# Attention in a diffusion backbone layer: the joint item of the four context heads moves from the middle of its group to the end of it

## The chip, the cores and the metric

The kernel runs on one core of a Trainium2 chip. Five engines of that core matter here: TensorE (PE, with PEld for its weight loads), VectorE (DVE), ScalarE (ACT), GpSimd (POOL) and SyncE (SP, which issues most DMAs). Each runs its own instruction stream and waits on semaphores that the others raise. The metric is the device time of one execution in microseconds. Before the change the median of 3 runs is 1314.7 us (1314.26 to 1314.91).

## The reference

One layer of a hybrid backbone for 512 latent tokens and 128 context tokens, D = 1024, 8 heads. After modulation and norm, one input projection feeds a gated convolution and a differential attention; both are merged, and a two-level routed mixture of experts follows. The part around the change is the attention: two softmaxes per head over the same keys, of which the second is subtracted with a factor.

```
def diff_attention(q, k, v, lam):          # q, k: (tokens, 8 heads, 2, 64)
    s = einsum('bqhcd,bkhcd->bchqk', q, k) / sqrt(64)
    p = softmax(s, axis=-1)
    a = p[:, 0] - lam * p[:, 1]
    return einsum('bhqk,bkhv->bqhv', a, v)  # v: (tokens, 8 heads, 128)
```

Latent queries (4 tiles of 128) attend to 640 keys: the 512 latent ones and 128 cached context ones. The 128 context queries attend only to their own 128 keys.

## The kernel before, in words

The kernel is written engine by engine, with semaphores by hand; no scheduler reorders anything. The heads are handled in two groups of four. A group first makes its queries and keys (line 1481, with the transposes at 1488), then runs attention, and then the next group begins. After group 1 the feature products (line 1595) follow; then the output projection, the router and 16 experts.

The attention of a group is a pipeline over 17 items. Sixteen are long items: one head times one tile of 128 latent queries, against 640 keys, with both softmaxes. One is the context item: all four heads of the 128 context queries together, against 128 keys. The place of the context item in the group is the constant `CTX_AT` (line 95), which `item(n)` (line 99) and `long_items(n)` (line 105) read; every engine's loop asks `item(n)` which kind item n is. Items are numbered 0 to 16 within a group here.

What one item costs each engine, with the lines:

- PE: scores into one half of a two-part PSUM area (L1532, four matmuls for a long item; L1523, eight small ones for the context item), transposes of the mixed probabilities (L1559, four; a long item has a fifth, L1565), and the product with the values (L1577, five matmuls of a long item; L1570, four of the context item).
- DVE: the maxima (L1051 long, L1047 context), the mix of the two softmaxes (L1032, L1033, L1036 long; L1022, L1023, L1027, L1029 context, which form one chain in which each waits for the one before), and the copy of the result out of PSUM with the scaling (L1016 long, L1013 context).
- ACT: the exponentials with their row sums (L767, two of 640 columns for a long item; L760, eight of 128 columns for the context item), and the copies of the transposed probabilities to SBUF (L743 for the first four, L747 for the fifth).

The order of the work is set by three loops. At its turn m, PE does:

```
transposes of item m (waits for its mix)
if m + 3 < ITEMS: scores(m + 3)        # waits for the exponentials of m + 1
fifth transpose of m, if long          # waits for the first copy of m
values product of m                    # waits for the result copy of m - 1
```

DVE goes round with the result copy of m - 3, the maxima of m, and the mix of m - 1. ACT does the first copy of m - 2, then the exponentials of m with the fifth copy of m - 2 inside them: after the first of two in a long item, after the second of eight in the context item (L756, L765). All three queues run in order.

After item 16 of group 0, PE waits until the last result is copied (line 1581) and then starts the queries of group 1. After item 16 of group 1 it does not wait for that: the next instruction is a transpose of a packed table (L1584), which waits only for something done long before, and then the feature products (L1595) begin.

Of the kernel before, what the change touches and what calls it, by code (L numbers as in the profile page):

```python
# [91 lines left out]
    return j if 0 <= j < 2 * NT else None  # L92


CTX_AT = 8
ITEMS = GROUP_HEADS * (NT - 1) + 1


def item(n):

    m = n % ITEMS
    return None if m == CTX_AT else divmod(m - (m > CTX_AT), NT - 1)


def long_items(n):

    return n - n // ITEMS - (n % ITEMS > CTX_AT)

# [1754 lines left out]
```

How the kernel before makes its waits and increments, by code:

```python
        def emptied(eng, j):  # L377
            who, count = EMPTIED[j]
            eng.wait_ge(s_emptied[who], count)
# [1 line left out]
        def job_done(eng, kind, n):  # L382
            eng.wait_ge(s_job, INDEX[(kind, n)] + 1)
# [11 lines left out]
        def more_chunks(eng, body):  # L395
            eng.wait_ge(s_meta, 1)
            total = eng.value_load(meta[0:1, 32:33], min_val=0, max_val=EXPERTS * CHUNKS)
            with eng.If(total > 0):
                with eng.Fori(0, EXPERTS) as e:
                    count = eng.value_load(meta[0:1, bass.ds(e, 1)], min_val=0, max_val=T)
                    base = eng.value_load(meta[0:1, bass.ds(e + 16, 1)], min_val=0, max_val=EXPERTS * CHUNKS)
                    with eng.Fori(1, CHUNKS) as c:
                        with eng.If(count > c * SLOTS):
                            body(e, c, base + c - 1)
# [5 lines left out]
            def load_chunk(n):  # L412
                if n >= W_SLOTS and CHUNK_LIST[n - W_SLOTS] == ("in", 10):
                    sp.wait_ge(s_vp, NT)
                elif n >= W_SLOTS:
                    sp.wait_ge(s_job, last_use(CHUNK_LIST[n - W_SLOTS]) + 1)
                sp.dma_start(slot[n % W_SLOTS].rearrange("p (k n) -> p k n", k=KT), chunk_src(CHUNK_LIST[n])).then_inc(s_w[n % W_SLOTS], 16)
# [20 lines left out]
            def load_feature(j):  # L438
# [2 lines left out]
                        "cv": ("conv", c), "at": ("attn", c)}[kind]  # L441
                if j < 2:
                    sp.wait_ge(s_job, last_use((("in", 9), ("ada", ADA_PAIRS[4][0]))[j]) + 1)
                else:
```

## Time and profile before

| | us |
|---|---|
| median of 3 runs | 1314.7 |
| the profiled execution's own time | 1314.13 |
| its span in the trace | 1312.3 |
| PE busy | 1257.6 (96%) |
| DVE busy | 564.9 (43%) |
| ACT busy | 233.7 (18%) |
| POOL busy | 284.8 (22%) |

The items of group 0 run from about 168 to 225 us of the span, those of group 1 from 347 to 404 us. The rest of the span is queries and keys, feature products, the output projection with the router, and the experts. The busy time of PE includes matmuls whose end is modelled, so a share of 96% doesn't say that the array does useful work all that time. The columns of a timeline row are the start, the duration, the engine, the line, the operation with its operands and the count; in square brackets stands how long the engine was idle before it and what released it.

### The profile page before, as it was taken

Reading aid. Unit: us, or ns where it says so; the run is one execution under the profiler, and the core shown is the slowest. Engines: PE = TensorE matmul, PEld = TensorE weight load, DVE = VectorE, ACT = ScalarE, POOL = GpSimd, SP = SyncE. Lnnn points to the kernel's source line nnn. Section 1 sums busy time; section 2 is a strip of 40 time slices with the busy share of each in tenths; the row PEclk is TensorE's granted clock in tenths of the full one; section 3 lists DMA queues with packets and bytes.
Section 4 is the critical chain, followed back from the end, with each engine's and each line's share of the span. In section 5 each row is a group of like instructions: output and inputs, shape, how many; then the busy total and the mean of one; then the engine's idle time right before and its main releaser. Section 6 shows DMA issues by size and latency. Waiting matters only on the chain.

```text
span 1312.3 us, 11731 instructions
## 1 busy us (share of the span) xinstructions
PE 1257.6 (96%) x4533; PEld 725.2 (55%) x4534; DVE 564.9 (43%) x999; ACT 233.7 (18%) x485; POOL 284.8 (22%) x205
## 2 busy tenths in 40 slices
PE   4999999999999999999999999999799999999995
PEld 1444466444576767767777777545444444444442
DVE  2312266444286783674255345365522222222222
ACT  3212265213372002001100110111110101010100
POOL 0223000443003333333233331000203131313121
PEclk9999999999999999999999999999999999999998
DMA  9752220013000111111221145311799888889751
GB/s 355 272 193 104 96 72 18 0 64 136 9 1 0 65 64 65 64 65 66 89 101 66 64 158 211 144 48 65 298 425 383 322 358 327 358 321 357 307 224 33
DMA packets 59284, 209.00 MB, mean 159 GB/s; under 512 B 8992, under 2 KB 9312, under 8 KB 53088
## 3 DMA queue, kind: packets, MB, share of 16 engines
q1 hardware_dynamic: 46480, 185.72, 36.6%
q0 software_dynamic: 12000, 20.48, 4.4%
q10 hardware_dynamic: 752, 2.11, 0.4%
q8 instruction: 33, 0.54, 0.2%
q14 instruction: 19, 0.16, 0.0%
HBM read 208.24 MB, written 23.10 MB: 176 GB/s over the span
## 4 chain that ended last, share of the span: by engine, by line
PE 88%; DVE 6%; issue 2%; ACT 1%; DMA 1%; SPq 1%; POOL 0%; POOLq 0%; DVEq 0%; ACTq 0%
PE psum L1595 30%; PE psum L1753 17%; PE psum L1481 11%; PE psum L1772 8%; PE psum L1543 5%; PE psum L1659 4%; PE psum L1532 3%; PE psum L1577 3%; PE psum L1434 2%; SPq L427 1%; DMA weight_ring<-in_w_ada 1%; DVE arena L1082 1%; PE psum L1732 1%; PE psum L1559 1%; DVE softmax_stats L1051 1%
## 5 line engine op out<-in xcount | busy, mean ns | idle before, releaser
L1595 PE MATMUL psum<-arena,weight_ring 128*128 128x320 f32 x928 | 256.9, 432 | 0.0
L1753 PE MATMUL psum<-weight_ring,arena 128*128 128x512 f32 x512 | 222.7, 593 | 0.7 <-ACT arena L840 0.7
L1595 PEld LDWEIGHTS psum<-arena,weight_ring 128*128 128x128 f32 x928 | 175.9, 190 | 72.7
L1595 PE MATMUL psum<-x,weight_ring 128*128 128x320 f32 x640 | 180.0, 433 | 2.1 <-DVE arena L1106 2.1
L1753 PEld LDWEIGHTS psum<-weight_ring,arena 128*128 128x128 f32 x512 | 96.1, 190 | 115.2 <-issue 114.3
L1595 PEld LDWEIGHTS psum<-x,weight_ring 128*128 128x128 f32 x640 | 120.9, 190 | 52.4 <-DVE arena L1106 3.1
L1481 PE MATMUL psum<-weight_ring,arena 128*128 128x512 f32 x320 | 140.6, 593 | 0.4 <-DVE arena L1016 0.4
L1772 PE MATMUL psum<-arena 128*128 128x512 f32 x256 | 112.6, 593 | 0.7 <-ACT arena L848 0.7
L584 POOL TENSOR_TENSOR weight_ring<-weight_ring 128x1024 f32<-128x1024 f32 x14 | 34.1, 2433 | 347.7 <-DMA weight_ring<-in_w_in 149.6
L1481 PEld LDWEIGHTS psum<-weight_ring,arena 128*128 128x128 f32 x320 | 59.4, 190 | 69.5 <-issue 68.5
L1106 DVE TENSOR_TENSOR arena<-psum,arena 128x320 f32<-128x320 f32 x124 | 59.4, 487 | 84.1 <-PE psum L1595 83.5
L1372 DVE SCALAR_TENSOR_TENSOR arena<-psum,ropeC,arena 128x512 f32<-128x512 f32 x16 | 12.0, 751 | 173.6 <-ACT arena L844 173.6
L1772 PEld LDWEIGHTS psum<-arena 128*128 128x128 f32 x256 | 47.5, 190 | 54.9 <-issue 54.0
L601 POOL DMA_INDIRECT y_sample<-arena,slot_rows_lat x16 | 19.3, 1205 | 259.8 <-DVE arena L1389 259.8
L1659 PE MATMUL psum<-weight_ring,arena 128*128 128x512 f32 x160 | 71.9, 598 | 2.0 <-DVE arena L1198 2.0
L1543 PE MATMUL psum<-weight_ring,arena 128*128 128x512 f32 x160 | 69.7, 595 | 0.0
L1434 PE MATMUL psum<-weight_ring,slot_one_hots 128*64 128x512 f32 x192 | 46.6, 637 | 17.2 <-DMA weight_ring<-in_w_ada 16.6
L808 ACT ACTIVATE ropeC<-psum 128x320 f32<-128x320 f32 x28 | 12.2, 437 | 266.4 <-PE psum L1595 227.8
L1106 DVE TENSOR_TENSOR arena<-psum,ropeC 128x320 f32<-128x320 f32 x40 | 19.6, 491 | 91.0 <-PE psum L1595 90.9
L767 ACT ACTIVATE arena<-psum,softmax_stats 128x640 f32<-128x640 f32 x64 | 50.7, 794 | 28.0 <-DVE softmax_stats L1051 28.0
L964 DVE TENSOR_REDUCE qkstat<-arena 128x8 f32<-128x512 f32 x20 | 13.7, 686 | 93.5 <-ACT arena L706 93.5
L1384 DVE TENSOR_TENSOR arena<-psum,arena 128x512 f32<-128x512 f32 x32 | 22.1, 691 | 71.9 <-PE psum L1772 71.9
(253 smaller groups left out, 1328.3 us busy)
## 6 DMA issues: line engine op xcount, KB each, us to landing
weight_ring<-in_w SPq DMA_DIRECT2D x32, 2048.0 KB, 12.0
weight_ring<-in_w_in SPq DMA_DIRECT2D x16, 2048.0 KB, 7.7
arena<-in_w SPq DMA_DIRECT2D x16, 2048.0 KB, 10.6
weight_ring<-in_w_ada SPq DMA_DIRECT2D x8, 2048.0 KB, 10.7
weight_ring<-in_w_ada SPq DMA_DIRECT2D x8, 1024.0 KB, 14.4
x<-in_x_sample SPq DMA_DIRECT2D x2, 2048.0 KB, 11.9
weight_ring<-in_w_conv_out SPq DMA_DIRECT2D x2, 2048.0 KB, 8.2
weight_ring<-in_w_attn_out SPq DMA_DIRECT2D x2, 2048.0 KB, 7.9
```

The costliest lines, as they stand in the source:

```text
L584: nc.gpsimd.tensor_tensor(made[:, 0], w21, w22, add).then_inc(s_fs, 1)
L767: last = A(prob[n % 2][:, c, :], S[:, KEYS * c:KEYS * (c + 1)], ACT.Exp, bias=st[:, c:c + 1], accum_out=st[:, 4 + c:5 + c])
L1106: return V.tensor_tensor(out, product_psum(q, name), value, add)
L1434: last = mm(ps[LANE * lane:LANE * (lane + 1), 0:512], lanes_c[:, k, :], w[:, k, :], start=(k == 0), stop=(k == KT - 1))
L1481: last = mm(ps[:, 0:512], hT[:, k, P * i:P * (i + 1)], w[:, k, :], start=(k == 0), stop=(k == KT - 1))
L1532: last = mm(psum[:, base + KEYS * c + lo:base + KEYS * c + hi], q, kT[64 * c:64 * (c + 1), h, key:key + hi - lo], start=True, stop=True)
L1543: last = mm(v_psum(i), hT[:, k, P * i:P * (i + 1)], w[:, k, :], start=(k == 0), stop=(k == KT - 1))
L1577: last = mm(psum[:, 3840:3968], aT[n % 2][:, P * j:P * (j + 1)], v_sb[:, j, P * h:P * (h + 1)], start=(j == 0), stop=(j == NT - 1))
L1595: last = mm(product_psum(q, name), w[:, k, :], src[:, k, :], start=(k == 0), stop=(k == 3))
L1659: last = mm(ps[:, 0:512], mixT[:, k, P * i:P * (i + 1)], w[:, k, :], start=(k == 0), stop=(k == KT - 1))
L1753: last = mm(psum[:, 1024 + 512 * j:1536 + 512 * j], xgT[:, t, :], w[:, t, :], start=(t == 0), stop=(t == KT - 1))
L1772: last = mm(psum[:, 2560 + 512 * half:3072 + 512 * half], hhT[:, t, :], w[:, t, 512 * half:512 * (half + 1)], start=(t == 0), stop=(t == 3))
```

## The change

One constant changes: the context item goes from place 8 to place 16 in each group, behind the sixteen long items. The long items of places 9 to 16 each come one place earlier. No instruction is added or dropped; every loop takes its kind of item from the same function.

```
-CTX_AT = 8
+CTX_AT = 16
 ITEMS = GROUP_HEADS * (NT - 1) + 1
 
 def item(n):
     m = n % ITEMS
     return None if m == CTX_AT else divmod(m - (m > CTX_AT), NT - 1)
```

On PE, at the turn of item 8 of group 0, this stands before (L1559 transposes, L1532 scores of item 11, L1570 the context item's values product):

```order
L1559 MATMUL psum<-ident,arena 128x128 x4
L1532 MATMUL psum<-arena 128x128
L1532 MATMUL psum<-arena 128x256
L1532 MATMUL psum<-arena 128x512
L1532 MATMUL psum<-arena 128x384
L1570 MATMUL psum<-arena 128x128 x4
L1559 MATMUL psum<-ident,arena 128x128 x4
```

and this with the change (L1565 is the fifth transpose and L1577 the values product of a long item):

```order
L1559 MATMUL psum<-ident,arena 128x128 x4
L1532 MATMUL psum<-arena 128x128
L1532 MATMUL psum<-arena 128x256
L1532 MATMUL psum<-arena 128x512
L1532 MATMUL psum<-arena 128x384
L1565 MATMUL psum<-ident,arena 128x128
L1577 MATMUL psum<-arena 128x128 x5
L1559 MATMUL psum<-ident,arena 128x128 x4
```

The context item is gone from this place, and a long one stands there. At the end of group 0 on PE, from the turn of item 14 on, before:

```order
L1559 MATMUL psum<-ident,arena 128x128 x4
L1565 MATMUL psum<-ident,arena 128x128
L1577 MATMUL psum<-arena 128x128 x5
L1559 MATMUL psum<-ident,arena 128x128 x4
L1565 MATMUL psum<-ident,arena 128x128
L1577 MATMUL psum<-arena 128x128 x5
L1559 MATMUL psum<-ident,arena 128x128 x4
L1565 MATMUL psum<-ident,arena 128x128
L1577 MATMUL psum<-arena 128x128 x5
L1481 MATMUL psum<-weight_ring,arena 128x512 x16
```

and from the turn of item 13 on, with the change (L1523 is the context item's scores):

```order
L1559 MATMUL psum<-ident,arena 128x128 x4
L1523 MATMUL psum<-arena 128x128 x8
L1565 MATMUL psum<-ident,arena 128x128
L1577 MATMUL psum<-arena 128x128 x5
L1559 MATMUL psum<-ident,arena 128x128 x4
L1565 MATMUL psum<-ident,arena 128x128
L1577 MATMUL psum<-arena 128x128 x5
L1559 MATMUL psum<-ident,arena 128x128 x4
L1565 MATMUL psum<-ident,arena 128x128
L1577 MATMUL psum<-arena 128x128 x5
L1559 MATMUL psum<-ident,arena 128x128 x4
L1570 MATMUL psum<-arena 128x128 x4
L1481 MATMUL psum<-weight_ring,arena 128x512 x16
```

The context item's scores come in the turn of item 13 and its values product directly ahead of the queries of group 1 (L1481). On ACT, at the end of group 0, from the first copy of item 14 (L743) and the exponentials of item 16 (L767) on, before:

```order
L743 ACTIVATE arena<-psum 128x512
L767 ACTIVATE arena,softmax_stats<-psum,softmax_stats 128x640
L747 ACTIVATE arena<-psum 128x128
L767 ACTIVATE arena,softmax_stats<-psum,softmax_stats 128x640
L743 ACTIVATE arena<-psum 128x512
L747 ACTIVATE arena<-psum 128x128
L743 ACTIVATE arena<-psum 128x512
L747 ACTIVATE arena<-psum 128x128
L706 ACTIVATE arena<-psum 128x512
```

and with the change, from the first copy of item 14 on too:

```order
L743 ACTIVATE arena<-psum 128x512
L760 ACTIVATE arena,context_softmax_stats<-psum,context_softmax_stats 128x128 x2
L747 ACTIVATE arena<-psum 128x128
L760 ACTIVATE arena,context_softmax_stats<-psum,context_softmax_stats 128x128 x6
L743 ACTIVATE arena<-psum 128x512
L747 ACTIVATE arena<-psum 128x128
L743 ACTIVATE arena<-psum 128x512
L706 ACTIVATE arena<-psum 128x512
```

The eight exponentials (L760) now stand between the first copies of items 14 and 15; the fifth copy of item 14 is inside them. POOL and SP keep their order, and the ends of group 1 look the same, with L1584 and L1595 in the place of L1481.

## Rows read from the trace of the kernel before

**Rows 1.** The page: span, and the chain that ended last, shares by engine.
```profile
span 1312.3 us, 11731 instructions
...
PE 88%; DVE 6%; issue 2%; ACT 1%; DMA 1%; SPq 1%; POOL 0%; POOLq 0%; DVEq 0%; ACTq 0%
```

**Rows 2.** Busy time by stretch: stretch, length, PE, PEld, DVE, ACT, POOL, clock, DMA.
```profile
184.99:199.16 14.17, 12.70 (x99) 9.74 (x98) 12.03 (x22) 10.68 (x36) 0.00 (x0) 1.00 0.00 0
199.16:212.82 13.66, 13.66 (x93) 10.18 (x94) 11.89 (x20) 9.71 (x25) 0.00 (x0) 1.00 0.01 2
212.82:225.39 12.57, 9.48 (x70) 7.51 (x68) 8.08 (x16) 7.00 (x18) 0.00 (x0) 1.00 0.01 2
363.79:377.96 14.17, 12.71 (x99) 9.76 (x97) 12.01 (x22) 10.69 (x36) 0.00 (x0) 1.00 0.01 2
391.62:403.59 11.97, 9.32 (x70) 7.54 (x69) 7.72 (x15) 7.01 (x18) 0.00 (x0) 1.00 0.00 0
```

**Rows 3.** Timeline, PE, 182 to 200: start, us, line, count, [idle before <- releaser].
```profile
184.99 0.60 PE L1559 MATMUL psum<-ident,arena 128*128 128x128 f32 x4
...
193.25 1.45 PE L1532 MATMUL psum<-arena 64*128 64x128 f32 x8 [1.05 <-ACT arena L760]
...
197.82 1.16 PE L1570 MATMUL psum<-arena 128*128 128x128 f32 x8
199.16 0.65 PE L1559 MATMUL psum<-ident,arena 128*128 128x128 f32 x4 [0.18 <-DVE arena L1036]
```

**Rows 4.** Timeline, ACT, 182 to 200, the context item's exponentials and what follows.
```profile
190.12 0.37 ACT L760 ACTIVATE arena<-psum,context_softmax_stats 128x128 f32<-128x128 f32 x1 [0.48 <-DVE context_softmax_stats L1047]
...
190.82 0.27 ACT L747 ACTIVATE arena<-psum 128x128 f32<-128x128 f32 x1
...
192.94 0.25 ACT L760 ACTIVATION_READ_ACCUMULATOR arena<-psum,context_softmax_stats 128x1 f32 x1
193.04 0.64 ACT L743 ACTIVATE arena<-psum 128x512 f32<-128x512 f32 x1
```

**Rows 5.** Timeline, DVE, 182 to 200, the context item's steps.
```profile
188.87 1.21 DVE L1047 TENSOR_REDUCE context_softmax_stats<-psum 128x8 f32<-128x1024 f32 x1
...
193.47 0.19 DVE L1022 RECIPROCAL context_softmax_stats<-context_softmax_stats 128x8 f32<-128x8 f32 x1
...
194.68 0.69 DVE L1029 TENSOR_TENSOR arena<-arena 128x512 f32<-128x512 f32 x1
...
199.02 0.69 DVE L1013 TENSOR_TENSOR arena<-psum,context_softmax_stats 128x512 f32<-128x512 f32 x1
```

**Rows 6.** Timeline, PE, 208 to 230, the end of group 0.
```profile
211.48 1.50 PE L1577 MATMUL psum<-arena 128*128 128x128 f32 x10
...
217.52 0.33 PE L1565 MATMUL psum<-ident,arena 128*128 128x128 f32 x1 [0.69 <-ACT arena L743]
...
219.32 0.49 PE L1577 MATMUL psum<-arena 128*128 128x128 f32 x2 [0.58 <-ACT arena L747]
219.65 0.60 PE L1559 MATMUL psum<-ident,arena 128*128 128x128 f32 x4
220.94 0.33 PE L1565 MATMUL psum<-ident,arena 128*128 128x128 f32 x1 [0.69 <-ACT arena L743]
...
225.39 4.99 PE L1481 MATMUL psum<-weight_ring,arena 128*128 128x512 f32 x11 [0.44 <-DVE arena L1016]
```

**Rows 7.** Timeline, PE, 391 to 404, the end of group 1.
```profile
402.48 1.28 PE L1577 MATMUL psum<-arena 128*128 128x128 f32 x10
403.59 0.27 PE L1584 MATMUL psum<-ident,rowpack 128*48 128x128 f32 x1
```

**Rows 8.** Timeline, PE, 925 to 962, a longer idle stretch in the routing part.
```profile
925.39 3.65 PE L1434 MATMUL psum<-weight_ring,slot_one_hots 128*64 128x512 f32 x16
...
933.92 0.67 PE L1695 MATMUL psum<-arena 128*128 128x80 f32 x4 [3.28 <-DVE arena L1289]
...
934.70 5.31 PE L1434 MATMUL psum<-weight_ring,slot_one_hots 128*64 128x512 f32 x16
```

**Rows 9.** Busy time by stretch, columns as in rows 2.
```profile
934.00:936.00 2.00, 2.00 (x10) 1.20 (x12) 1.23 (x9) 0.00 (x0) 0.59 (x1) 0.66 0.03 10
```

More of the change, by code:

```diff
@@ L92, in oT_step @@
     return j if 0 <= j < 2 * NT else None
-CTX_AT = 8
+CTX_AT = 16
 ITEMS = GROUP_HEADS * (NT - 1) + 1
```

## The prediction

> **What bounds the kernel now.** I read the page first: the chain that ended last runs 88% of the 1312.3 us span over PE [rows 1], so a change counts where PE idles or is made to idle. Next the timeline of PE through both attention groups, with what each idle stretch waits for, then the same stretch on ACT and DVE, and last the busy time by stretch.
>
> Four long items in a row, 199.16 to 212.82 us, take 13.66 us, 3.415 us each, with PE busy all the time [rows 2]. That is not PE's own pace. The values product of a long item is recorded as 1.50 us there (at 211.48) [rows 6], and as 1.28 us where nothing holds it [rows 7]. The 0.22 us are a hidden wait of its last matmul for the fifth copy, which on ACT stands behind an exponential, which stands behind the DVE maxima, which stand behind the last result copy. So a long item could pass PE in about 3.20 us, and the ring over the three engines makes it 3.415.
>
> The context item now disturbs the four turns 5 to 8, from 184.99 to 199.16 us: 14.17 us, of which PE is busy 12.70 [rows 2]. The largest idle piece is 1.05 us, where scores wait for the eight exponentials [rows 3]. At the group's end PE idles for other reasons: no scores are left to put between a transpose and the product that needs its copy. From the start of item 13's transposes (212.82) to the first matmul of group 1's queries (225.39) is 12.57 us, 9.48 of them busy [rows 2].
>
> **The middle.** With the change turns 5 to 8 are four long ones, at the pace of their neighbours: 13.66 us in place of 14.17 [rows 2], so −0.51 us in group 0. Group 1 shows 14.17 too (363.79 to 377.96) and gives the same. That is less than the 1.47 us of idle that vanish, since with a long item in that place the hidden waits come back and the cheaper scores and product go.
>
> **The end of group 0.** I count from Z, the start of item 13's transposes, when the context item's scores are next on PE. That is just what turn 5 does before the change, at 184.99 [rows 3], so offsets from 184.99 carry over to the first steps.
>
> ACT: the first context exponential starts at 190.12, Z + 5.13; the fifth copy of item 14, inside them, at Z + 5.83; the last sum is read out at 193.19, Z + 8.20; and the next item's first copy, queued behind all eight, starts at 193.04, Z + 8.05 [rows 4].
>
> PE: item 14's product tail can start when that fifth copy ends, 0.27 + 0.04 us later, at Z + 6.14, and item 15's transposes 0.33 us after that (219.32 to 219.65 [rows 6]), at Z + 6.47. They last 0.60 us, so they end at Z + 7.07, and now PE idles until item 15's first copy is made. That starts at Z + 8.05 and lasts 0.60 to 0.64 us (PE resumes 0.05 later), so item 15's fifth transpose starts at Z + 8.71 and PE idles 1.64 us there, against 0.69 before [rows 6]. The product follows 0.16 us later, 1.28 us long [rows 7], and ends at Z + 10.15.
>
> DVE: it takes up the context mix when the last sum is read, Z + 8.24. From the reciprocal (193.47) to the end of the last step (194.68 + 0.69) that takes 1.90 us [rows 5], so to Z + 10.14. PE, then just through with item 15, starts item 16's transposes at Z + 10.19. They are recorded as 0.65 us after such a wait [rows 3], then 0.69 us pass until the copy is there [rows 6], so the context product starts at Z + 11.53, takes 1.16 [rows 3] and ends at Z + 12.69. Its result copy on DVE takes 0.69 us (199.02 [rows 5]) with 0.04 us at each end, and PE waits for it before the queries: Z + 13.46.
>
> So 13.46 in place of 12.57, +0.89 us; with the middle, +0.38 us for group 0.
>
> **The end of group 1.** The same up to Z + 11.53. Nothing waits here for the result copy: L1584 follows the start of the last product by 1.11 us where this is 1.28 long [rows 7], so by 0.99 where it is 1.16: Z + 12.52, against 11.97 now [rows 2]. +0.55 − 0.51 = +0.04 us. The longer result copy lies under the first feature products.
>
> What is behind both groups starts from PE, which is the chain there, so I pass the shifts on in full. No DMA and no POOL instruction changes its place.
>
> **Sum.** +0.38 + 0.04 = +0.42 us: span 1312.7 in place of 1312.3, the profiled execution 1314.55 in place of 1314.13, and the median 1315.1 in place of 1314.7, which lies 0.6 above the profiled execution before and is assumed to do so again. Bounds of what the trace doesn't show: the last two turns with a context item in them. At the least they idle no more than the present end, plus only the longer copy (0.69 for 0.35, so +0.34 once): −1.02 + 0.34 = −0.7 us. At the most none of the context item's work at the end overlaps the long ones: the exponentials (3.07 us), the mix (1.90) and the product (1.16) stand beside what the last long item's product takes now (1.28), +4.9 per group, less 0.51: +8.7 us for both. The first end leaves out a queue that rows 4 show, the second forgets that item 15 runs under the mix; I take the step by step count.
>
> **Weighed: PE's clock.** In every stretch of rows 2 the granted clock is 1.00, the 2.4 GHz level. In the routing part, after PE sat idle for 3.28 us (to 933.92), it is 0.66 over the next 2 us [rows 8, 9], a mix of 2.4 and 1.2 GHz, and the 16 matmuls of L1434 take 5.31 us there in place of 3.65. The new idle pieces at the end of a group are 1.6 and 0.8 us at most, with matmuls between them.
> The Trainium skill (TensorE: Matmul & The Clock Gate, Part 1) says that the slow clock is the default and only activity lifts it, which speaks against putting the item where PE has the least to do. The trace agrees as to the long idle stretch, and shows none of 1.6 us with a lower clock. By the rule taken strictly the sum would be the third case below, by the rows alone it is +0.42.
>
> **Rivals.**
> 1. The end costs nothing more: item 15's copy comes early or is covered, and only the middle counts, −1.02 us, or with all 1.47 us of idle gone in both groups −2.9 us: 1311.8 to 1313.7. For it: the ring's hidden waits could shrink. Against it: ACT's order puts eight exponentials ahead of item 15's copy, and the neighbours of the context item run at 3.415 us on either side. 4% for −1.02 and about, 1% for beyond −2.6.
> 2. The end is longer than counted, through the mix chain meeting DVE's other work or a copy that starts late, +1 to +2 us: 1315.7 to 1316.7. For it: three engines take turns there. Against it: each step is taken from its own row, and DVE has nothing else but two result copies. 11%.
> 3. The clock falls at the end of a group. The place is the first queries of group 1 (L1481) and the first feature products. Its price by rows 8 is 5.31 − 3.65 = 1.66 us an occurrence, so 2 × 1.66 + 0.42 = +3.7 us: 1318.4, slower than before. It decides once PE's idle of 1.6 us next to a thinly filled stretch is enough. 4%.
> 4. The change doesn't do what it says, that is, the time stays where it was because the item's work moves and nothing else; 0 ± 0.2 us. It would need the middle and the end to cancel, 8%.
>
> **How the numbers follow.** The forecast, +0.1 to +0.8 us, has 72%; 1 to 4 have 5, 11, 4 and 8%. A measurement of this kernel can tell about 0.2%, 2.6 us, from no change. Faster by that needs the far end of case 1: 1%, and 1% for what I don't see. Slower by that is case 3 with the far bound: 5%. The rest, 93%, is within 0.2%. The range takes in cases 1 (its near part), 2 and 4 and the spread of the runs of before (0.65 us): 1313.6 to 1316.6.
>
> **What the changed profile would show.** Right: no idle before L1532 released by L760; turns 0 to 13 at 3.4 us throughout; about 1.6 us of idle before item 15's L1565, released by L743; L1022 released by L760 after DVE idled over 1 us; L1570 last in the group, and some 0.8 us of idle before L1481, released by L1013. Wrong: a gap over 2 us at the group's end, a clock under 1.00 behind it, or turns other than 3.4 us in the middle.

## The result, and the profile after

| | before | with the change |
|---|---|---|
| median, us | 1315.24 (20 runs) | 1316.64 (20 runs) |
| lowest to highest | 1314.26 to 1317.12 | 1315.37 to 1321.20 |
| mean, us | 1315.43 | 1317.35 |
| span of the profiled execution | 1312.3 | 1315.8 |

The ratio is 1.0015, with a 95% interval of 1.0008 to 1.0022: slower by 1.1 to 2.9 us, about 2.0 (the medians lie 1.4 us apart, the means 1.9). The forecast was 1315.1 in a range of 1313.6 to 1316.6, +0.42 us. The direction was right and the size wrong, by a factor of three (medians) to nearly five (ratio). The median lies just outside the range, by 0.04 us; how near it is to the edge means little, since the median of 3 runs that the range was built on (1314.7) was 0.5 us under that of 20. The table shows more than the medians do: the lowest time rose by 1.1 us and the highest by 4.1. Something in the changed kernel happens in some executions and not in others. The mean granted clock of each run goes with it: the four runs above 1319 us have 0.988 or 0.989 of full speed, the three from 1317.3 to 1317.8 have 0.990 or 0.991, and the thirteen up to 1317.14 have 0.992 to 0.994.

The end of group 0 on PE, in the profiled execution after the change. The columns are those of [rows 6]. The count behind x is one of records: an attention product or a query matmul has two (the context item's four matmuls are x8), a transpose has one.

```profile
212.55 0.60 PE L1559 MATMUL psum<-ident,arena 128*128 128x128 f32 x4
...
221.29 0.33 PE L1565 MATMUL psum<-ident,arena 128*128 128x128 f32 x1 [1.66 <-ACT arena L743]
221.46 2.20 PE L1577 MATMUL psum<-arena 128*128 128x128 f32 x10
223.45 1.06 PE L1559 MATMUL psum<-ident,arena 128*128 128x128 f32 x4
225.19 1.16 PE L1570 MATMUL psum<-arena 128*128 128x128 f32 x8 [0.69 <-ACT arena L743]
227.13 5.42 PE L1481 MATMUL psum<-weight_ring,arena 128*128 128x512 f32 x12 [0.78 <-DVE arena L1013]
```

Item 13's transposes start at 212.55 (Z). The idle piece ahead of item 15's fifth transpose is 1.66 us, as forecast (1.64), and the fifth transpose is at Z + 8.74 (forecast 8.71). But then item 15's product takes 2.20 us, where a free one takes 1.28 [rows 7], and the four transposes behind it 1.06 in place of 0.65 [rows 3]. The rows of the clock show PE at half its speed there. The stretches of this execution, with the columns of [rows 2] (length, busy times, then the granted clock):

```profile
220.00:222.00 2.00, 0.71 (x5) 0.71 (x6) 1.12 (x3) 1.52 (x7) 0.00 (x0) 0.90 0.00 0
222.00:224.00 2.00, 2.00 (x11) 2.00 (x11) 1.00 (x2) 0.00 (x0) 0.00 (x0) 0.50 0.00 0
224.00:226.00 2.00, 1.31 (x10) 0.91 (x9) 0.04 (x1) 0.60 (x1) 0.00 (x0) 0.74 0.00 0
226.00:228.00 2.00, 1.22 (x6) 0.65 (x5) 0.69 (x1) 0.00 (x0) 1.07 (x2) 1.00 0.00 0
924.00:926.00 2.00, 2.00 (x13) 1.46 (x14) 1.68 (x10) 1.29 (x4) 0.00 (x0) 0.69 0.90 377
```

The clock is 0.50 of full over 222 to 224 us, the 1.2 GHz level, and back at 1.00 from 226. In [rows 2] it is 1.00 in every stretch shown. At the end of group 1 of this same execution, behind an idle piece of 1.66 us too, it stays at 1.00. At 924 to 926 it is low too, behind an idle piece of 1.59 us which the kernel before has as well and over which its clock stayed at 1.00 in the profiled execution.

From this the 3.5 us between the two spans divide as follows, by the starts of the same rows in both chains of waits: +0.27 at the first scores, a start that differs by chance; +1.47 in group 0 (227.13 against 225.39, less 0.27); +0.06 in group 1; −0.17 in the feature products; +1.82 between the output projection and the first expert, where the clock was low for longer than in the execution before. Only the group terms belong to the change. The order of work gives +0.38 of the +1.47, and the clock the rest, 1.1 us.

### The profile page after: what moved, and what is told of

It is laid out like the page before. It is cut to its first block, busy times and chain, and to the rows that moved or that the text cites. A ratio compares the mean times of both kernels' runs of the same rounds, so it can differ in the third digit from the quotient of the medians.

```text
span 1315.8 us, 11731 instructions
## 1 busy us (share of the span) xinstructions
PE 1262.3 (96%) x4533; PEld 728.3 (55%) x4534; DVE 562.2 (43%) x999; ACT 233.5 (18%) x485; POOL 284.5 (22%) x205
## 4 chain that ended last, share of the span: by engine, by line
PE 89%; DVE 5%; issue 2%; ACT 1%; DMA 1%; SPq 1%; POOL 0%; POOLq 0%; DVEq 0%; ACTq 0%
PE psum L1595 30%; PE psum L1753 17%; PE psum L1481 10%; PE psum L1772 8%; PE psum L1543 5%; PE psum L1659 4%; PE psum L1532 3%; PE psum L1577 3%; PE psum L1434 2%; SPq L427 1%; DMA weight_ring<-in_w_ada 1%; DVE arena L1082 1%; PE psum L1732 1%; PE psum L1559 1%; PE psum L1488 1%
## 5 line engine op out<-in xcount | busy, mean ns | idle before, releaser
L1595 PE MATMUL psum<-arena,weight_ring 128*128 128x320 f32 x928 | 256.9, 432 | 0.0
L1595 PEld LDWEIGHTS psum<-arena,weight_ring 128*128 128x128 f32 x928 | 175.9, 190 | 72.7
L1595 PE MATMUL psum<-x,weight_ring 128*128 128x320 f32 x640 | 180.0, 433 | 1.9 <-DVE arena L1106 1.9
L1595 PEld LDWEIGHTS psum<-x,weight_ring 128*128 128x128 f32 x640 | 120.9, 190 | 52.2 <-DVE arena L1106 3.0
L1481 PE MATMUL psum<-weight_ring,arena 128*128 128x512 f32 x320 | 140.6, 593 | 0.8 <-DVE arena L1013 0.8
L1481 PEld LDWEIGHTS psum<-weight_ring,arena 128*128 128x128 f32 x320 | 59.4, 190 | 69.8 <-issue 68.5
L1106 DVE TENSOR_TENSOR arena<-psum,arena 128x320 f32<-128x320 f32 x124 | 59.4, 487 | 85.1 <-PE psum L1595 84.5
L1543 PE MATMUL psum<-weight_ring,arena 128*128 128x512 f32 x160 | 69.7, 595 | 0.0
L1434 PE MATMUL psum<-weight_ring,slot_one_hots 128*64 128x512 f32 x192 | 46.9, 640 | 17.5 <-DMA weight_ring<-in_w_ada 16.9
L1106 DVE TENSOR_TENSOR arena<-psum,ropeC 128x320 f32<-128x320 f32 x40 | 19.7, 491 | 92.0 <-PE psum L1595 91.8
L767 ACT ACTIVATE arena<-psum,softmax_stats 128x640 f32<-128x640 f32 x64 | 50.7, 795 | 29.3 <-DVE softmax_stats L1051 29.3
```

The source lines that it names most:

```text
L767: last = A(prob[n % 2][:, c, :], S[:, KEYS * c:KEYS * (c + 1)], ACT.Exp, bias=st[:, c:c + 1], accum_out=st[:, 4 + c:5 + c])
L1106: return V.tensor_tensor(out, product_psum(q, name), value, add)
L1434: last = mm(ps[LANE * lane:LANE * (lane + 1), 0:512], lanes_c[:, k, :], w[:, k, :], start=(k == 0), stop=(k == KT - 1))
L1481: last = mm(ps[:, 0:512], hT[:, k, P * i:P * (i + 1)], w[:, k, :], start=(k == 0), stop=(k == KT - 1))
L1543: last = mm(v_psum(i), hT[:, k, P * i:P * (i + 1)], w[:, k, :], start=(k == 0), stop=(k == KT - 1))
L1595: last = mm(product_psum(q, name), w[:, k, :], src[:, k, :], start=(k == 0), stop=(k == 3))
```

## The experiments

All times are compared with runs of the kernel before, made on the same chip at the same time. "Before" had 15 to 33 runs there, with medians of 1315.05 to 1315.36 us. The theory after the result: the order of work costs +0.42 us as worked out, and the thin stretch at a group's end lets PE's clock fall in some executions. The rival: the group ends are innocent and the excess comes from the routing part (900 to 960 us of the span), whose clock falls now and then in any version. Line numbers in rows of an edited kernel lie a few lines further on than those of before, where lines were added ahead of them.

### E1: the changed kernel again

No edit.

> The changed kernel once more, untouched. Both theories have the same order of work, +0.42 us: -0.51 and +0.89 in group 0, -0.51 and +0.55 in group 1. Clock theory: the idle at a group's end (1.66, 0.69 and 0.78 us) now and then lets PE's clock fall to its lower level there, in some executions and not in others, so the times spread upward: median +1 to +2 us over before, and a trace shows either a stretch under 1.00 behind the context item or none. Rival, the routing theory: the end of the groups keeps its clock nearly always, and what is over +0.42 comes from the routing part (900 to 960 us of the span), whose own dips in the clock are drawn anew with every shift of the start; then before and after spread alike.

Measured: median 1317.70 (1315.00 to 1320.43, 11 runs), ratio 1.0019 (1.0010 to 1.0028). The profiled execution was the fastest of them, 1315.00 us, and its clock is 1.00 at both group ends. It shows the order of work alone. PE at the end of group 0, and then in a second fence at the end of group 1:

```profile
212.28 0.60 PE L1559 MATMUL psum<-ident,arena 128*128 128x128 f32 x4
...
221.01 0.33 PE L1565 MATMUL psum<-ident,arena 128*128 128x128 f32 x1 [1.65 <-ACT arena L743]
...
222.47 0.66 PE L1559 MATMUL psum<-ident,arena 128*128 128x128 f32 x4
223.81 1.16 PE L1570 MATMUL psum<-arena 128*128 128x128 f32 x8 [0.69 <-ACT arena L743]
225.75 4.56 PE L1481 MATMUL psum<-weight_ring,arena 128*128 128x512 f32 x10 [0.78 <-DVE arena L1013]
```

```profile
391.47 0.60 PE L1559 MATMUL psum<-ident,arena 128*128 128x128 f32 x4
...
404.00 0.27 PE L1584 MATMUL psum<-ident,rowpack 128*48 128x128 f32 x1
```

Counted from Z = 212.28: the fifth transpose of item 15 at Z + 8.73 (forecast 8.71), item 16's transposes at Z + 10.19 (10.19), the context product at Z + 11.53 (11.53), group 1's queries at Z + 13.47 (13.46). In group 1 L1584 comes at Z + 12.53 (12.52). So the step count was right to 0.02 us, and what was wrong lies outside it. The spread is upward, as the clock theory said: the mean granted clock is 0.994 in the four runs up to 1316.1 us and 0.988 to 0.992 in the seven above. The 33 runs of before have 0.991 to 0.995.

### E2: the idle at the group ends filled

```
+ def filler(count, bank):      # identity times itself, into PSUM that nobody reads
+     for _ in range(count):
+         mm(psum[:, bank:bank + P], ident[:, :], ident[:, :], start=True, stop=True)
                    if m + 3 < ITEMS:
                        scores(n + 3)
+                   filler({ITEMS - 2: 6, ITEMS - 1: 2}.get(m, 0), 1536 * ((start + ITEMS - 2) % 2))
                    pe.wait_ge(s_aT, n + 1)
...
                if g == 0:
+                   filler(3, 1536 * ((start + ITEMS - 2) % 2))
                    pe.wait_ge(s_o, ITEMS)
```

> The changed kernel, with small matmuls of the identity by itself put into the idle stretches of the last turns (6 while item 15's first copy is awaited, 2 for item 16's, 3 before group 1's queries in group 0). They write PSUM that nobody reads and add no wait; their results are not used. Each lasts about 0.22 us, so they fit into the idle time: order of work +0.4 to +0.6 us over before. Clock theory: the granted clock stays 1.00 at both ends of the groups, time +0.4 to +0.8 us over before and the upward tail is gone, 1 to 1.5 us faster than the changed kernel. Routing theory: like the changed kernel, +1.4 to +2 us over before.

Measured: median 1315.75 (1314.13 to 1317.05), ratio 1.0001 (0.9992 to 1.0010). Extra work on PE made the kernel 2 us faster than E1, on the same chip. The end of group 0 on PE (L1548 are the added matmuls) has the rows of E1, with the idle pieces down to 0.31 and 0.24 us:

```profile
212.53 0.60 PE L1563 MATMUL psum<-ident,arena 128*128 128x128 f32 x4
...
219.45 1.50 PE L1548 MATMUL psum<-ident 128*128 128x128 f32 x12
221.26 0.33 PE L1570 MATMUL psum<-ident,arena 128*128 128x128 f32 x1 [0.31 <-ACT arena L743]
...
224.07 1.16 PE L1575 MATMUL psum<-arena 128*128 128x128 f32 x8 [0.24 <-ACT arena L743]
...
226.01 4.56 PE L1481 MATMUL psum<-weight_ring,arena 128*128 128x512 f32 x10
```

The queries start at Z + 13.48 (Z = 212.53), as in E1. The order of work is the same, the clock is 1.00 at both group ends, and the upward tail is gone: six of E1's eleven runs lie above E2's highest. Against the kernel before E2 is no gain; it takes back what the change lost.

### E3: the context item first

```
-CTX_AT = 16
+CTX_AT = 0
```

> The context item at place 0 instead of 8 or 16. Its exponentials then run on ACT while PE computes the values, its product comes in the first turn. The middle saves 0.5 us a group as in the changed kernel, the end is as before the change (12.57 and 11.97 us from item 13 on), and the first turn is 0.2 us shorter. Both theories: -1.2 to -1.6 us against before, with the clock at the group's ends as before. If the time doesn't fall, the saving of the middle is not what the trace shows.

Measured: median 1313.95 (1312.85 to 1314.61), ratio 0.9989 (0.9980 to 0.9998), as expected. The middle's saving is real when nothing is paid for it at the end: the exponentials run on ACT from 132.57 to 135.3 us, while PE is busy with the matmuls that make the values (L1543). A piece of it goes to a wait of 0.30 us for the fifth copy in the turn after the context item.

### E4: the idle alone, without the context item

The kernel before, with ACT held up ahead of item 15's first copy:

```
+                   if n - ITEMS * g == ITEMS - 2:
+                       for b in range(2):
+                           A(qk_s[b], psum[:, 3072:3072 + N_LAT], ACT.Copy)
                    A(aT[n % 2][:, 0:N_LAT], psum[:, 3072:3072 + N_LAT], ACT.Copy).then_inc(s_aT, 1)
```

> The kernel before (context item in the middle), with two more PSUM copies of 512 columns on ACT ahead of item 15's first copy, into a buffer that isn't in use; results unchanged. PE's idle before item 15's fifth transpose grows from 0.69 to about 1.8 us at each group's end, without any context item there: order of work +2.2 to +2.4 us over before. Clock theory: the clock falls behind it in some executions as in the changed kernel, median +3 to +4 us and a spread upward. Routing theory: +2.2 to +2.4 us and no dip at the ends.

Measured: median 1317.75 (1315.96 to 1318.72), ratio 1.0016 (1.0007 to 1.0025). The end of group 0 grew by 0.98 us (13.55 for 12.57), so the order of work is +2.0, and the median +2.45 is hardly more. The expected size (+3 to +4 us in the median, with a spread upward) was too large: the mean granted clock is 0.993 to 0.995 in every run, no lower than those of before. Its trace shows the effect itself all the same, on PE at the end of group 1:

```profile
401.95 0.47 PE L1568 MATMUL psum<-ident,arena 128*128 128x128 f32 x1 [1.67 <-ACT arena L746]
402.22 2.34 PE L1580 MATMUL psum<-arena 128*128 128x128 f32 x10
404.35 1.06 PE L1562 MATMUL psum<-ident,arena 128*128 128x128 f32 x4
```

Behind 1.67 us of idle the product takes 2.34 us and the transposes 1.06. So the clock can fall there with the context item in the middle; how often it does can't be read from this.

### E5 and E6: one idle piece filled, or the others

E5 has only the 6 matmuls ahead of item 15's fifth transpose, E6 only those behind it (2, and 3 in group 0).

> The changed kernel with the small matmuls only where item 15's first copy is awaited (6 of them, in the 1.65 us of idle); the later idle pieces stay as they are. Their results are not used. Order of work +0.4 us over before. If the longest idle piece alone makes the clock fall: like the version with everything filled, 0 to +0.6 us over before, no upward tail. If the whole thin stretch does, with the two idle pieces of 0.69 and 0.78 us behind it: between that and the changed kernel, +1 us with some upward tail.

> The changed kernel with the small matmuls only behind item 15: 2 while item 16's first copy is awaited, 3 before the queries of group 1. The 1.65 us of idle ahead stay. If the longest idle piece alone makes the clock fall: like the changed kernel, +1.5 to +2.5 us over before, reaching above 1319. If the whole thin stretch does: +1 us over before, the tail shorter.

Measured: E5 median 1315.43 (1314.38 to 1317.30), ratio 1.0003 (0.9994 to 1.0012). E6 median 1314.80 (1313.91 to 1315.99), ratio 0.9996 (0.9987 to 1.0005). E5 came out as expected of one case, E6 as of neither: with the longest idle piece left in, the tail was gone too. E6's profiled execution (1315.84 us, its second slowest) has a short fall, in three stretches at the end of group 1 (columns of [rows 2], the clock third from the end):

```profile
400.00:402.00 2.00, 1.58 (x8) 1.58 (x9) 1.73 (x4) 0.65 (x2) 0.00 (x0) 0.64 0.00 0
402.00:404.00 2.00, 2.00 (x11) 2.00 (x11) 0.35 (x1) 0.15 (x1) 0.00 (x0) 0.51 0.00 0
404.00:406.00 2.00, 1.89 (x15) 1.61 (x14) 0.30 (x1) 0.64 (x2) 0.00 (x0) 1.00 0.03 8
```

The clock did fall behind the 1.65 us, but PE had no further idle to speak of and was at 1.00 again by 404 us; L1584 (L1590 here) came 1.3 us later than without a fall. That the long piece starts a fall and the thin work behind it draws it out fits this trace, but it is argued from one execution. What E5 and E6 show is that filling either part takes the upward tail away.

### E7 and E8: the routing part filled, in the changed kernel and in the one before

```
+           filler(6, 512)
            x2_T(2 * NT - 1)
...
            rank(NT - 1)
+           filler(13, 512)
            table(NT - 1)
```

> The changed kernel with small matmuls in the two idle stretches of the routing part (6 in the 1.59 us, 13 in the 3.27 us), their results not used, and the group ends as changed. The clock then stays up in the routing part, so what spread is left comes from the group ends. Clock theory: still 3 us and more between the lowest and the highest time, median +1.5 to +2 us over the next kernel. Routing theory: the spread is gone, and the median is +0.4 us over the next kernel.

> The kernel before (context item at place 8) with the same matmuls in the routing part. The clock stays 1.00 from 900 to 960 us, where it fell to 0.5 for about 3 us: 1.5 to 2 us faster than before, 1313.0 to 1313.8, and the times lie within 1 us of each other. If they spread as before, the routing part isn't where before's own spread comes from.

Measured: E8 median 1314.08 (1313.91 to 1315.56, ten of eleven within 0.5 us), ratio 0.9992 (0.9983 to 1.0001). E7 median 1315.70 (1314.27 to 1319.49), ratio 1.0005 (0.9996 to 1.0014). So most of the spread of the kernel before comes from the routing part, and that of the changed kernel doesn't: with the routing part filled, its median is 1.6 us over E8's, as the clock theory said (+1.5 to +2), its lowest time 0.36 us over E8's, and it reaches 5.2 us above that. The trace of E7 has a low clock at the end of group 1, in these stretches:

```profile
400.00:402.00 2.00, 1.41 (x9) 1.41 (x10) 1.81 (x4) 0.81 (x3) 0.00 (x0) 0.78 0.00 0
402.00:404.00 2.00, 1.61 (x8) 1.21 (x7) 0.35 (x1) 0.35 (x1) 0.00 (x0) 0.50 0.00 0
404.00:406.00 2.00, 1.70 (x8) 1.71 (x9) 0.00 (x0) 0.24 (x1) 0.00 (x0) 0.50 0.03 8
406.00:408.00 2.00, 2.00 (x7) 1.37 (x7) 0.69 (x1) 0.27 (x1) 0.00 (x0) 0.51 0.00 0
```

L1584 (L1588 here) comes 1.8 us later behind this than at full clock. There is a second fall in the same execution, at 489 to 493 us in the feature products; E11 shows that place again. E8 gained less than expected (1.0 for 1.5 to 2 us), with PE waiting 1.58 us for the first gathered tokens behind the filled pieces.

### E9: late, but not last

```
-CTX_AT = 16
+CTX_AT = 12
```

> The context item at place 12: still late, but item 15's scores and its copies come after the context exponentials, so the end of the group (from item 14 on) is as before. Order of work: the middle's four turns of 14.17 us move four places later, the end is unchanged: 0 us against before (1315.1), spread as before. If it is slower by 1 us or more, lateness as such costs, and not the last places.

Measured: median 1315.43 (1314.29 to 1317.09), ratio 1.0000 (0.9991 to 1.0009). As expected. Lateness costs nothing that these runs can tell, as long as the last items behind it are long.

### E10: item 15's first copy ahead of three of the exponentials

```
                                    last_probs_T(n - 2)
+                               if (c, h) == (1, 1) and n == start + ITEMS - 1:
+                                   probs_T(n - 1)
...
-                   probs_T(n - 2)
+                   if m != ITEMS or item(n - 1) is not None:
+                       probs_T(n - 2)
```

> The changed kernel, with item 15's first copy taken out of its place behind the eight context exponentials and put behind the fifth of them. By the step count of the prediction: the copy starts at Z + 7.1 in place of Z + 8.05 and PE idles 0.7 us ahead of it in place of 1.65, but the last sum comes 0.6 us later, so the mix ends at Z + 10.75 and the order of work is 0.6 us a group longer than in the changed kernel: +1.6 us over before. PE idles some 1.2 us ahead of item 16's transposes instead. Clock theory: what comes on top is less than in the changed kernel if the longest idle piece decides, and the same if the sum does.

Measured: median 1321.90 (1321.80 to 1322.63, 5 runs), ratio 1.0053 (1.0039 to 1.0066), four times what the order of work says. All five runs have it. The end of group 0 on PE: item 14's transposes (L1562), item 15's product (L1580), item 16's transposes (L1562), the context product (L1573) and the queries (L1484). Then the stretches with their clock:

```profile
216.04 0.60 PE L1562 MATMUL psum<-ident,arena 128*128 128x128 f32 x4
...
220.57 1.54 PE L1580 MATMUL psum<-arena 128*128 128x128 f32 x10
223.40 1.11 PE L1562 MATMUL psum<-ident,arena 128*128 128x128 f32 x4 [1.29 <-DVE arena L1032]
225.20 2.07 PE L1573 MATMUL psum<-arena 128*128 128x128 f32 x8 [0.69 <-ACT arena L743]
228.05 16.75 PE L1484 MATMUL psum<-weight_ring,arena 128*128 128x512 f32 x32 [0.78 <-DVE arena L1016]
```

```profile
222.00:224.00 2.00, 0.71 (x4) 0.61 (x4) 1.57 (x3) 0.00 (x0) 0.00 (x0) 0.85 0.00 0
226.00:228.00 2.00, 1.27 (x6) 0.97 (x5) 0.69 (x1) 0.00 (x0) 0.15 (x1) 0.50 0.00 0
230.00:232.00 2.00, 2.00 (x4) 0.93 (x3) 0.00 (x0) 0.00 (x0) 0.00 (x0) 0.50 0.41 164
232.00:240.00 8.00, 8.00 (x18) 3.41 (x17) 0.69 (x1) 1.99 (x3) 0.00 (x0) 0.90 0.00 0
```

In group 1, where the clock stayed at 1.00, L1587 (the L1584 of other versions) comes 0.6 us later than in E1, as worked out. In group 0 the queries start 1.35 us later than worked out (Z + 15.42, with Z = 212.63, for Z + 14.07), and their first 16 matmuls (32 records) take 16.75 us in place of 14.00, since the clock is still at 0.50 when they begin and stays there past 232 us, with PE busy all the time. And the longest idle piece here is 1.29 us, shorter than the 1.65 of the changed kernel, and yet the five times are above all 31 of that kernel: the length of the longest piece alone isn't what decides. Only one of the five executions has a trace; that the others fell in the same place is not shown, though their mean granted clock (0.988 to 0.990) is as low.

### E11 and E12: two combinations

E11 has the context item at place 0 and the routing part filled as in E8. E12 is the changed kernel with both the group ends and the routing part filled.

> The context item at place 0, with the small matmuls in the two idle stretches of the routing part as in e7 and e8 (their results not used). The two gains should add: -1.3 us of e3 on the 1314.1 us of e8: 1312.7 to 1312.9 us, with times within 1 us of each other.

> The changed kernel with the small matmuls both at the ends of the groups (as in e2) and in the routing part (as in e7), their results not used. If the clock at the group ends is all that came on top of the order of work, the times are those of e8 (before, routing part filled: 1314.1 us) plus 0.4 us, 1314.3 to 1314.6, within 1 us of each other, where e7 reached from 1314.3 to 1319.5. If it is something else about the changed end, the upward tail of e7 stays.

Measured: E11 median 1313.06 (1312.82 to 1316.56, nine of eleven up to 1313.39), ratio 0.9987 (0.9978 to 0.9996). E12 median 1315.20 (1314.39 to 1318.16), ratio 1.0003 (0.9994 to 1.0012). E11's median is 0.2 us above what was expected, and two runs reach up, which was not. Its profiled execution (1314.88 us) is one of the two, and its clock is 1.00 at the group ends and in the routing part. It fell in the feature products, where PE waits for DVE (L1106) in every version. The row of the kernel before, and then that of E11 (L1599 is L1595 of before):

```profile
485.42 4.57 PE L1595 MATMUL psum<-x,weight_ring 128*128 128x320 f32 x16 [1.88 <-DVE arena L1106]
```

```profile
484.31 6.26 PE L1599 MATMUL psum<-x,weight_ring 128*128 128x320 f32 x16 [1.88 <-DVE arena L1106]
```

The clock of E11 is 0.50 over 486 to 488 us, and the fall costs 1.69 us. E7's row is the same (6.26 us behind 2.01 of idle), and the other sixteen traces are at full clock there. So there is a third place where the clock falls now and then, with the context item at any place. No experiment here fills it, so part of the tails that are left in the filled versions may come from it.

E12's median is higher than expected, and a tail remained. Its trace is at 1.00 at both group ends and low (0.63 over 940 to 944 us) in yet another place, where PE's timeline reads:

```profile
941.20 1.94 PE L1740 MATMUL psum<-ident,arena 128*128 128x128 f32 x8 [2.30 <-DMA arena<-h_scratch,slot_tokens]
```

The filling of the routing part had opened a piece of 2.30 us ahead of the first gathered tokens, and the clock fell there: the eight transposes take 1.94 us, where the kernel before has 1.16. The comparison was not clean, so it was made again with that piece filled too (E13 to E15).

### E13 to E16: three pieces filled behind the output projection, on one chip

```
+           filler(8, 512)
            tokens_T(0, s_xg[0], 16, 0)
```

This on top of the edit of E7, in the kernel before (E13), the changed one (E14), the changed one with its group ends filled (E15), and the one with the context item first (E16).

> The kernel before with small matmuls in three idle pieces behind the output projection: the two of e7 and e8, and 8 more where PE waits for the first gathered tokens. Their results are not used. No clock below 1.00 between 900 and 960 us; 1313.9 to 1314.4, as e8 or tighter.

> The changed kernel with the same three fillings, the ends of the groups left idle. If the group ends' clock is the cause: the lowest time 0.4 us over e13's lowest, and a spread of 3 to 6 us above it. If not: e13 plus 0.4 us without a tail.

> The changed kernel with the same three fillings and the ends of the groups filled as in e2. If the group ends' clock is the cause: e13's times plus 0.4 us, at most one of the runs over 1 us above the median. If something else about the changed end costs: the tail of e14 stays.

> The context item at place 0 with the same three fillings: e13's times less 1.1 to 1.3 us, 1312.7 to 1313.1. The best version of this study if both gains add.

| | median | lowest to highest | ratio (95%) |
|---|---|---|---|
| E13 before | 1315.11 | 1314.48 to 1316.06 | 0.9996 (0.9987 to 1.0005) |
| E14 changed | 1317.15 | 1314.48 to 1319.71 | 1.0009 (0.9999 to 1.0019) |
| E15 changed, ends filled | 1315.48 | 1315.03 to 1317.07 | 1.0001 (0.9992 to 1.0010) |
| E16 first | 1313.48 | 1313.14 to 1316.41 | 0.9986 (0.9977 to 0.9995) |

E13 came out at 1315.11 us, 0.25 under before, where 1313.9 to 1314.4 was expected. E15 over E13 is +0.37 us in the median and +0.7 in the mean, which is in line with the order of work (+0.42 worked out) but too coarse to confirm it; E1's rows do that. Two of E15's runs lie over 1 us above its median, where at most one was expected. E14 over E15 is +1.67 us in the median and 2.6 in the highest, and the only difference between the two is the filling at the group ends: six of E14's eleven runs lie above E15's highest, as six of E1's lie above E2's. E14's lowest time equals E13's, where 0.4 more was expected; within the scatter of 1.6 us that E13 has on this chip, where E8 had 0.5 for ten of its eleven runs, that says nothing. E14's profiled execution has a span of 1317.5 us, and its end of group 0 on PE reads:

```profile
221.41 0.33 PE L1569 MATMUL psum<-ident,arena 128*128 128x128 f32 x1 [1.65 <-ACT arena L743]
221.57 1.28 PE L1581 MATMUL psum<-arena 128*128 128x128 f32 x10
222.87 1.00 PE L1563 MATMUL psum<-ident,arena 128*128 128x128 f32 x4
224.56 2.07 PE L1574 MATMUL psum<-arena 128*128 128x128 f32 x8 [0.69 <-ACT arena L743]
227.42 16.89 PE L1481 MATMUL psum<-weight_ring,arena 128*128 128x512 f32 x32 [0.79 <-DVE arena L1013]
```

The clock in the stretches of the same execution:

```profile
222.00:224.00 2.00, 1.86 (x12) 1.26 (x10) 1.13 (x3) 0.14 (x2) 0.00 (x0) 0.76 0.00 0
224.00:226.00 2.00, 1.44 (x6) 1.44 (x7) 0.00 (x0) 0.51 (x1) 0.00 (x0) 0.50 0.00 0
228.00:230.00 2.00, 2.00 (x3) 0.67 (x2) 0.00 (x0) 0.00 (x0) 0.29 (x1) 0.50 0.69 219
230.00:240.00 10.00, 10.00 (x21) 4.35 (x20) 0.93 (x3) 2.18 (x3) 0.00 (x0) 0.84 0.02 9
```

The product right behind the 1.65 us of idle still runs at full speed (1.28 us); the clock falls during item 16's transposes. From there to the queries takes 4.55 us (222.87 to 227.42), against 3.28 in E1, and the queries' first 16 matmuls 16.89 against 14.00: 1.3 + 2.9 = 4.2 us from one fall. E15's profiled execution has no stretch under 1.00 from the first item to the first expert and a span of 1313.3 us, 4.2 less than E14's, so this one fall is the whole difference between the two.

E16 is faster than both kernels, by 1.9 us against before in the median, with a ratio of 0.9986 (expected: 1312.7 to 1313.1, 1.1 to 1.3 us under E13; measured: 1.6 under E13, which itself was slower than expected); E11's 0.9987 agrees, and E3, which needs no filling, has 0.9989.

## Why the prediction was wrong

The order of work was right. The four turns of the middle run at 3.41 us each like their neighbours, which makes the 0.51 us less a group, and the ends came out at Z + 13.47 and Z + 12.53 for 13.46 and 12.52 (E1). Each sign that the prediction named for its being right is in the profile after: no idle ahead of the scores released by L760, 1.66 us ahead of item 15's L1565, L1022 after 1.20 us of idle on DVE, and 0.78 us ahead of L1481. So is one that it named for its being wrong: a clock under 1.00 behind the end of the group (0.50 over 222 to 224 us).

The step that failed is the one headed "Weighed: PE's clock", with rival 3, "The clock falls at the end of a group", which got 4%, so the sum has no term for it. It argued that the trace shows no idle piece of 1.6 us with a lower clock behind it. That was true of the one execution it had. The routing part of the changed kernel is that of before, and in its profiled execution the clock is 0.69 over 924 to 926 us, behind the piece of 1.59 us that left it at 1.00 before. Executions of the kernel before differ too, for E8 took away most of its spread by filling the pieces of 1.59 and 3.27 us. One profile without a fall does not show that there will be none in the next execution. What the runs show in place of the 4%: behind the 1.65 us the clock fell at the end of one group in the profiled execution and in the traces of E6, E7 and E14, not in that of E1, and six of eleven runs of E1, and again of E14, lie above the highest time that the same kernel has with its group ends filled (E2, E15).

The size of rival 3 was off too. Its 1.66 us an occurrence came from the L1434 rows [rows 8], with dense work right behind the gap. At the end of group 0 it is 1.1 us when the clock comes back ahead of the queries (the profiled execution) and 4.2 when it doesn't (E14). And it was priced as certain in both groups, 3.7 us in all, where it comes in some executions: the median of the changed kernel lies 1.0 us above the order of work by the first 20 runs (1316.64 less 1315.24 and 0.42), the mean 1.5 us, and the highest times over 5.

In hindsight: a mean of +2 us would have come out of the prediction's own parts, had the case been given an even chance, though it would have been luck, since the price was wrong as well. What spoke for a higher chance was in the rows: 9.48 us busy of 12.57 at the end before the change [rows 2], about to become thinner (9.17 of 13.47 in E1).

Rivals 1, 2 and 4 did not happen. The end costs what the steps say, so nothing was covered (1) and nothing was longer (2); the middle and the end do not cancel, since E1's rows have +0.90 and +0.56 at the ends against −0.51 each (4).

The Trainium skill (TensorE: Matmul & The Clock Gate, A second HAM failure mode: psum-queue depth-cycling) tells of another kernel, in bf16, where PE idling briefly but often between groups of matmuls makes the clock go back and forth. The prediction took from the same part of that page only that activity lifts the clock, and went by the longest idle piece. The traces agree that short pieces can do it: no piece at the group ends is over 1.67 us, and in E10 none is over 1.29. A clock that goes back and forth within one group end is in none of them; each trace has at most one fall there.

Still open is what makes one execution fall and the next not. The runs show that the clock falls in some executions of the same instructions, and that filling either the first or the later pieces takes the upward tail away (E5, E6). They don't show why E10 fell in all five, or why E4, with idle pieces like those of the changed kernel, lost hardly anything on top.

## What to carry to other kernels

An item with a long chain through the other engines belongs where the matrix engine has dense work that covers it: here at the start, under the matmuls that make the values, and not among the last items, where each engine waits for the next. When a reordering thins out a stretch, the sum of the steps is only its lower end; add the case that the clock falls there, priced by the work behind it that runs slow, and look at the spread of the times and at each run's mean granted clock before trusting one clean profile. If the stretch can't be made dense, matmuls in the idle time that nobody reads can pay for themselves (E2 against E1: 2 us). All of this is about 0.1 to 0.2% of this kernel, so single runs can't show it.

## What the runs showed of the hardware that was not expected

A low clock outlives the idle that began it. In E14 it was 0.50 or a mix of both levels from 222 us to somewhere past 230, although PE was busy without a break from 227.4 on, and the dense queries paid 2.9 us. In the profiled execution of the changed kernel, with the same instructions at the group's end, it was back at 1.00 by 226, ahead of the queries. The times of the one changed kernel reach from 1315.4 to 1321.2 us; its slowest runs have no trace, only their lower mean clock.
